# Sine arguments of a state-space mixer made in its front; one score product per head; softmax sums behind the scan; the exponential's table asked for before the score

## The reference, cut to what matters

```python
lam_bar = jnp.exp(lam * step)                      # one complex number per state
bu = jnp.einsum('blgh,gph->blgp', u_c, b_bar)
_, states = lax.associative_scan(_scan_combine, (a, bu), reverse=reverse, axis=1)
y = jnp.real(jnp.einsum('blgp,ghp->blgh', states, c))
...
s1 = jnp.einsum('bqhd,bkhd->bhqk', q_blk[..., 0, :], k1) + bias     # s2 alike
attn = jax.nn.softmax(s1, axis=-1) - lam * jax.nn.softmax(s2, axis=-1)
```

## Time and profile before

| what | us |
|---|---|
| median of 3 runs | 1440.96 |
| lowest and highest run | 1439.4, 1441.56 |
| span of the profiled execution, first to last instruction | 1437.0 |
| PE busy in the span | 1348.0 (94%) |
| DVE busy | 875.8 (61%) |
| ACT busy | 694.7 (48%) |
| POOL busy | 135.4 (9%) |

### The profile page before, as it was taken

One profiled execution on the slowest core, in us unless ns is written; L12 is line 12 of the kernel. 1 busy time (PEld: TensorE's weight loads), 2 busy tenths in 40 slices (PEclk: granted clock), 3 DMA queues, 4 the chain that ended last, 5 costly groups with the idle time before them and its releaser, 6 DMA issues.

```text
span 1437.0 us, 19125 instructions
## 1 busy us (share of the span) xinstructions
PE 1348.0 (94%) x7246; PEld 980.9 (68%) x7246; DVE 875.8 (61%) x1138; ACT 694.7 (48%) x1023; POOL 135.4 (9%) x111
## 2 busy tenths in 40 slices
PE   6996889999899779899999999999999999999996
PEld 6865558888787555776766667676766666666663
DVE  6888754454398875666565665555665555665552
ACT  4568443434246863445454544454444444444442
POOL 0455200000006640000000000000000000000000
PEclk9997999999899889899999999999999999999999
DMA  8541325443643126699999999999999999999993
GB/s 347 173 171 34 126 106 215 177 175 124 265 125 117 63 66 236 258 411 390 410 421 421 421 421 419 410 421 422 420 422 421 408 420 421 421 421 420 421 421 164
DMA packets 66329, 435.58 MB, mean 303 GB/s; under 512 B 8192, under 2 KB 14720, under 8 KB 16576
## 3 DMA queue, kind: packets, MB, share of 16 engines
q1 hardware_dynamic: 64848, 429.60, 74.4%
q0 software_dynamic: 1392, 4.78, 1.0%
HBM read 429.11 MB, written 2.10 MB: 300 GB/s over the span
## 4 chain that ended last, share of the span: by engine, by line
PE 73%; DMA 9%; DVE 9%; ACT 5%; SPq 2%; issue 2%; ACTq 0%; DVEq 0%
PE ps L2208 19%; PE ps L2243 11%; PE ps L2194 9%; PE ps L2096 7%; PE ps L1863 6%; PE ps L2225 6%; PE ps L2075 4%; DMA raw<-wmoe 4%; DMA first_ring<-wmoe 4%; PE ps L2001 2%; PE ps L1978 2%; SPq L548 2%; DVE raw L1321 1%; PE ps L1901 1%; PE ps L1989 1%
## 5 line engine op out<-in xcount | busy, mean ns | idle before, releaser
L2096 PE MATMUL ps<-wsplit,xh 128*128 128x512 f32 (+1 forms) x352 | 111.4, 388 | 5.0 <-DVE hv L1388 3.4
L1398 DVE TENSOR_TENSOR low_raw<-raw,last_uppers 128x2048 fp32r<-128x2048 f32 x39 | 89.2, 2289 | 38.5 <-ACT last_uppers L839 38.5
L1398 DVE TENSOR_TENSOR low_first<-first_ring,first_uppers 128x2048 fp32r<-128x2048 f32 x31 | 70.8, 2291 | 37.8 <-ACT first_uppers L839 37.8
L2243 PE MATMUL ps<-raw,hn 128*64 128x256 f32 x784 | 92.4, 382 | 0.0
L1863 PE MATMUL ps<-hT,mixw 128*128 128x256 f32 x384 | 89.4, 394 | 3.1 <-DMA mixw<-wmix 2.2
L1398 DVE TENSOR_TENSOR low_raw<-raw,first_uppers 128x2048 fp32r<-128x2048 f32 x31 | 70.8, 2289 | 32.6 <-ACT first_uppers L839 32.6
L1668 DVE TENSOR_TENSOR hv<-hv,ps 128x256 f32<-128x256 f32 x56 | 23.6, 421 | 105.3 <-ACT hv L989 105.3
L1362 DVE TENSOR_TENSOR wsplit<-raw,wsplit 128x2048 fp32r<-128x2048 f32 x33 | 74.5, 2289 | 20.1 <-ACT wsplit L798 20.1
L1863 PEld LDWEIGHTS ps<-hT,mixw 128*128 128x128 f32 x384 | 75.0, 198 | 15.2 <-issue 2.5
L2243 PE MATMUL ps<-last_ring,hn 128*64 128x256 f32 x704 | 83.2, 382 | 0.0
L989 ACT ACTIVATE hv<-ps 128x256 f32<-128x256 f32 x56 | 21.5, 384 | 127.5 <-PE ps L2208 127.5
(11 more groups left out here) (352 smaller groups left out, 3013.0 us busy)
## 6 DMA issues: line engine op xcount, KB each, us to landing
raw<-wmoe SPq DMA_DIRECT2D x148, 1024.0 KB, 22.4
first_ring<-wmoe SPq DMA_DIRECT2D x95, 1024.0 KB, 23.4
last_ring<-wmoe SPq DMA_DIRECT2D x91, 1024.0 KB, 23.2
raw<-wdense SPq DMA_DIRECT2D x33, 1024.0 KB, 5.0
mixw<-wmix SPq DMA_DIRECT2D x12, 2048.0 KB, 8.3
cyt<-bmat SPq DMA_DIRECT2D x2, 2048.0 KB, 12.1
cw<-cmat SPq DMA_DIRECT2D x2, 2048.0 KB, 18.4
qk<-wglu SPq DMA_DIRECT2D x2, 1024.0 KB, 5.0
```

What stands on the lines that cost most here:

```text
L1398: tt(lows[at], ring[at], uppers[k % UPPERS].bitcast(F32), ALU.subtract).then_inc(s["lo_done"], 1)
L2096: ins = mm(to, x2[:, fx, t * P:(t + 1) * P], of, start=(fx == 0 and i == 0), stop=(fx == KT - 1 and i == 2))
L2243: ins = mm(to, xlight[:, m % 2, fx], of[:, :, q * P:(q + 1) * P], start=(fx == 0), stop=(fx == KT - 1), tile_position=(0, LCAP * q))
```

## The change

It touches the mixer of both layers and nothing else.

1. The arguments of all 16 steps are made ahead of the loop, in four parts of 4, 4, 3 and 5 steps (`TURN_STEPS`): ACT's `phases` as two copies per step instead of four instructions, all 32 ahead of the eviction of zu1; one `nearest` per part (1024, 1024, 768, 1280 columns), and one `fracs` per part on DVE: part 0 ahead of `fold_c`, parts 1 and 2 behind it, part 3 in step 1. They lie in memory that v, hn and qk use later, and in a new tile `late`.
2. The shifted argument is gone: cos comes as the sine of (pi/2 - 2 pi |x|), so `trigs` is an Abs and three sines of 256 columns, the last behind a wait for the Abs.
3. `score` takes both least values of a head, then one product over 4 columns by a tensor_tensor with the slope from a column (four new memsets at the start), and gives one signal for both maps; `sums` multiplies by tensor_tensor too and stands behind the scan of its step.
4. ACT does a one-column exponential ahead of its wait for the score.
5. ACT waits for `frac_ready` in steps 1 and 2, and for `trig_ready` before the first eviction into v, because of the shared memory.

```diff
@@ -64,6 +64,7 @@
 STEPS = max(GP + 3, ATN_AT[-1] + 3)
+TURN_STEPS = (4, 4, 3, 5)
...
-        phase = sb("phase", [P, 2, SEQ])
-        turns = sb("turns", [P, 2, 2, SEQ])
+        late = sb("late", [P, 5, SEQ])
...
+        turn_parts = (v[:].rearrange("p t n -> p (t n)"), hn[:, 0], hn[:, 1, 0:3 * SEQ],
+                      late[:].rearrange("p i t -> p (i t)"))
+        whole_parts = [qk[:].rearrange("p a h t -> p (a h t)")[:, at:at + n * SEQ] for at, n in ((0, 4), (4 * SEQ, 4), (0, 3), (3 * SEQ, 5))]
...
@@ ScalarE @@
-            def phases(l, i):
-
-                n = GP * l + i
-                act.wait_ge(s["small_dve"], 2 * l + 2)
-                if n:
-                    act.wait_ge(s["frac_ready"], n)
-                for d in range(2):
-                    turn = small[:, 4, 2 * i + d:2 * i + d + 1]
-                    c = slice(d * NCH, (d + 1) * NCH)
-                    nc.scalar.activation(phase[:, 0, c], cst[:, C_T:C_T + NCH], ACT.Copy, scale=turn)
-                    ins = nc.scalar.activation(phase[:, 1, c], cst[:, C_T:C_T + NCH], ACT.Identity, bias=col[:, 17:18],
-                                               scale=turn)
...
+            def phases(l, b):
+
+                if b == 0:
+                    act.wait_ge(s["small_dve"], 2 * l + 2)
+                first = sum(TURN_STEPS[:b])
+                for i in range(first, first + TURN_STEPS[b]):
+                    for d in range(2):
+                        ins = nc.scalar.activation(turns_of(i)[:, d * NCH:(d + 1) * NCH], cst[:, C_T:C_T + NCH], ACT.Copy,
+                                                   scale=small[:, 4, 2 * i + d:2 * i + d + 1])
+                chain[0] += 1
+                phases_done[b] = chain[0]
+                ins.then_inc(s["act_chain"], 1)
+
+            def nearest(l, b):
+
+                act.wait_ge(s["act_chain"], phases_done[b])
+                if b >= 2:
+                    act.wait_ge(s["frac_ready"], len(TURN_STEPS) * l + b - 1)
+                nc.scalar.activation(whole_parts[b], turn_parts[b], ACT.Copy, bias=ROUND).then_inc(s["phase_ready"], 1)
...
-                nc.scalar.activation(trig[:, n % 3, 0], turns[:, i % 2, 1], ACT.Sin, scale=-TWOPI)
-                if between:
-                    between()
-                nc.scalar.activation(trig[:, n % 3, 1], turns[:, i % 2, 0], ACT.Sin, scale=-TWOPI)
-                nc.scalar.activation(trig[:, n % 3, 2], turns[:, i % 2, 0], ACT.Sin,
-                                     scale=TWOPI).then_inc(s["trig_ready"], 1)
+                chain[0] += 1
+                nc.scalar.activation(trig[:, n % 3, 0], turns_of(i), ACT.Abs).then_inc(s["act_chain"], 1)
+                nc.scalar.activation(trig[:, n % 3, 1], turns_of(i), ACT.Sin, scale=-TWOPI)
+                nc.scalar.activation(trig[:, n % 3, 2], turns_of(i), ACT.Sin, scale=TWOPI)
+                act.wait_ge(s["act_chain"], chain[0])
+                nc.scalar.activation(trig[:, n % 3, 0], trig[:, n % 3, 0], ACT.Sin, bias=col[:, 16:17],
+                                     scale=-TWOPI).then_inc(s["trig_ready"], 1)
...
                     if h >= 2:
                         full(unit(l, f"turn{h - 2}"))
+                    else:
+                        act.wait_ge(s["trig_ready"], GP * l + sum(TURN_STEPS[:h + 2]))
+                    nc.scalar.activation(col[:, 89:90], col[:, 17:18], ACT.Exp)
+                    act.wait_ge(s["score_ready"], HEADS * l + h + 1)
                     for m in range(2):
-                        act.wait_ge(s["score_ready"], 2 * (HEADS * l + h) + m + 1)
...
                 phases(l, 0)
+                phases(l, 1)
                 nearest(l, 0)
                 for k in range(2):
+                    if k:
+                        nearest(l, 1)
+                        phases(l, 2)
+                        phases(l, 3)
                     u = unit(l, "zu", k)
...
-                phases(l, 1)
-                trigs(l, 0, lambda: nearest(l, 1))
+                nearest(l, 2)
+                trigs(l, 0)
                 for i in range(STEPS):
-                    if i + 2 < GP:
-                        phases(l, i + 2)
-                        trigs(l, i + 1, lambda: nearest(l, i + 2))
-                    elif i + 1 < GP:
+                    if i + 1 < GP:
                         trigs(l, i + 1)
+                    if i == 0:
+                        nearest(l, 3)
+                    if i in (1, 2):
+                        act.wait_ge(s["frac_ready"], len(TURN_STEPS) * l + i + 2)
...
@@ VectorE @@
-            def fracs(l, i):
-
-                n = GP * l + i
-                dve.wait_ge(s["phase_ready"], n + 1)
-                stt(turns[:, i % 2], turns[:, i % 2], ROUND, phase[:], ALU.subtract,
-                        ALU.subtract).then_inc(s["frac_ready"], 1)
+            def fracs(l, b):
+
+                dve.wait_ge(s["phase_ready"], len(TURN_STEPS) * l + b + 1)
+                stt(turn_parts[b], whole_parts[b], ROUND, turn_parts[b], ALU.subtract,
+                    ALU.subtract).then_inc(s["frac_ready"], 1)
...
-            def score(l, h, m):
-
-                u = unit(l, f"map{h}.{m}")
-                full(u)
-                c, least = 64 + 4 * (h % 2) + 2 * m, col[:, 34 + 2 * m:36 + 2 * m]
-                at_least(dve, "score_ready", 2 * (HEADS * l + h) + m - 1)
-                link(nc.vector.tensor_reduce(least, ps[:, bank(u)].rearrange("p (a t) -> p a t", a=TT), axis=AX.X, op=ALU.min))
-                ts(col[:, c:c + 2], least, SLOPES[h], None, ALU.mult).then_inc(s["score_ready"], 1)
+            def score(l, h):
+
+                c = 64 + 4 * (h % 2)
+                at_least(dve, "score_ready", HEADS * l + h)
+                for m in range(2):
+                    u = unit(l, f"map{h}.{m}")
+                    full(u)
+                    ins = nc.vector.tensor_reduce(col[:, 34 + 2 * m:36 + 2 * m], ps[:, bank(u)].rearrange("p (a t) -> p a t", a=TT),
+                                                  axis=AX.X, op=ALU.min)
+                link(ins)
+                tt(col[:, c:c + 4], col[:, 34:38], col[:, 24 + h:25 + h].to_broadcast([P, 4]), ALU.mult).then_inc(s["score_ready"], 1)
...
-                ts(col[:, 82 + c:84 + c], col[:, 82 + c:84 + c], col[:, 14:15], None, ALU.mult).then_inc(s["sums_ready"], 1)
+                tt(col[:, 82 + c:84 + c], col[:, 82 + c:84 + c], col[:, 14:15].to_broadcast([P, 2]),
+                   ALU.mult).then_inc(s["sums_ready"], 1)
...
                 turn_b(l)
+                fracs(l, 0)
                 fold_c(l)
-                if l == 0:
-                    dve.wait_ge(s["in_cst"], 16)
-                fracs(l, 0)
                 fracs(l, 1)
+                fracs(l, 2)
                 stack = Stack(None)
                 for i in range(STEPS):
...
-                    for h in range(HEADS):
-                        if i == HEAD_AT[h] + T_SUMS:
-                            sums(l, h)
                     if i < GP:
                         rotate_in(l, i)
                         add_in(l, i)
                         scan(l, i)
-                    if i + 2 < GP:
-                        fracs(l, i + 2)
+                    for h in range(HEADS):
+                        if i == HEAD_AT[h] + T_SUMS:
+                            sums(l, h)
+                    if i == 1:
+                        fracs(l, 3)
```

More of the change, by code:

```diff
@@ L453, in at_least, with turn_part, turns_of @@
                 eng.wait_ge(s[what], n)
+        def turn_part(i):
+            return next(b for b in range(len(TURN_STEPS)) if i < sum(TURN_STEPS[:b + 1]))
+        def turns_of(i):
+            b = turn_part(i)
+            at = (i - sum(TURN_STEPS[:b])) * SEQ
+            return turn_parts[b][:, at:at + SEQ]
         @block.sync
@@ L718, in norm_empty @@
                     ins.then_inc(s["emptied_act"], 1)
-            def phases(l, i):
-                n = GP * l + i
-                act.wait_ge(s["small_dve"], 2 * l + 2)
-                if n:
-                    act.wait_ge(s["frac_ready"], n)
-                for d in range(2):
-                    turn = small[:, 4, 2 * i + d:2 * i + d + 1]
-                    c = slice(d * NCH, (d + 1) * NCH)
-                    nc.scalar.activation(phase[:, 0, c], cst[:, C_T:C_T + NCH], ACT.Copy, scale=turn)
-                    ins = nc.scalar.activation(phase[:, 1, c], cst[:, C_T:C_T + NCH], ACT.Identity, bias=col[:, 17:18],
-                                               scale=turn)
-                chain[0] += 1
-                ins.then_inc(s["act_chain"], 1)
@@ L735, in nearest @@
-            def nearest(l, i):
-                act.wait_ge(s["act_chain"], chain[0])
-                if GP * l + i >= 2:
-                    act.wait_ge(s["trig_ready"], GP * l + i - 1)
-                nc.scalar.activation(turns[:, i % 2], phase[:], ACT.Copy, bias=ROUND).then_inc(s["phase_ready"], 1)
-            def trigs(l, i, between=None):
-                n = GP * l + i
```

(17 more changed lines are left out.)

## The result

The changed kernel took 1435.56 us (median of seven runs, 1426.08 to 1438.02) against 1441.46 us before (seven runs, 1439.4 to 1449.35). By the medians the change is faster by 5.9 us where 17 were forecast, and 1435.56 lies above the range. Its own runs spread over 12 us, those of before, but for one, over 3; a second set of twelve runs of the same kernel gave 1432.46. The profiled execution ran 1436.12 us and its span is 1434.3, so it stands for the slower part of the runs, to which the median belongs.

A forecast was written before the change was run, and what follows sets the result against it. PE bounds each mixer's start (full to 104 us in layer 0), then DVE and ACT releasing each other up to the head norm. Layer gains 8.55 and 8.3, 16.85, called 17: median 1440.96 to 1424; range 1418 to 1430, full 1417 to 1432.

The forecast's parts named there:

- The front, a cost: Mixer start: PE begins 0.85 us late in layer 0, `local` 1.1 late in layer 1; bounds 0 to 2.5 a layer.
- I let all of it move with the end of the ring: Output projection, feed-forward and expert parts after the mixer: all start earlier by the mixer's gain, hiding none of it.
- The ring: Mixer steps up to the head norm, where DVE and ACT release each other's work: gains 8.55 us in layer 0, 8.3 in layer 1.
- To score(1): Mixer up to head 1's score: DVE stops being late and waits for PE's maps; 2.45 us gained, layer 0's late start included.
- Score(1) to score(2): Head 1's score to head 2's: 13.89 us falls to 11.1, gain 2.8, or 1.9 after 0.9 of waits beside POOL.
- Score(2) to rotation 13: Head 2's score to step 13's rotation: 10.56 us falls to 7.8, gain 2.75, less 0.6 of waits beside POOL.
- Rotation 13 to score(3): Step 13's rotation to head 3's score: 4.95 us falls to 3.46 without the subtraction, gain 1.5.
- Score(3) to the head norm: Head 3's score to the mixer's head norm: 12.54 us falls to 11.6, gain 0.95, less 0.4 of waits beside POOL.
- Holds: Score's and sums' new products on DVE wait beside POOL instructions: 0 to 1.27 us each, 1.9 a layer.
- Abs: Rival, in `trigs`: Abs outside sine's table adds two loads per `trigs`, 11 us a layer; 1446 us, chance 0.05.
- PE's order: Rival: both front delays fall on PE in each layer and the gain up to score(1) vanishes; 1429 us, chance 0.14.
- a ring held elsewhere: Rival, steps 10 to 15: POOL's pair ends last, about 13 us instead of 11 a pair; 1432 us, chance 0.12.

The follow-up runs named there:

- the gap filled: Changed kernel, with layer 1's second input product's eight matmuls repeated twice on PE, unread, ahead of the real ones: 1426.07 us, ratio 0.9902.
- the late C in the kernel before: Kernel before the change, with one of `fold_c`'s products made twice in layer 1 (2.2 us more DVE work): 1453.77 us, ratio 1.0108.
- C first: Changed kernel with part 0's subtraction moved behind `fold_c` in both layers: 1428.09 us, ratio 0.9924.
- the late C filled: Kernel before the change, with one `fold_c` product made twice in layer 1 and sixteen repeated input matmuls on PE: 1444.87 us, ratio 1.0037.
- Six dummies at the dense start: Changed kernel with part 0's subtraction behind `fold_c`, part 3's copies behind zu1's and B's evictions, six unread matmuls at the dense start: 1429.99 us.
- the head part: Kernel before the change, plus only one-product score, sums behind the scan and the exponential's load ahead: 1442.12 us, ratio 1.0018.
- the argument part alone: Changed kernel's new front and `trigs`, part 0 behind `fold_c`; score, sums and exponential's load as before the change: 1427.54 us, ratio 0.9916.

## Why the prediction was wrong

**The step that failed is "The front, a cost".** It priced C's delay as time: part 0's subtraction ahead of `fold_c`, 1.1 us. The delay is there: from the dense part's last addition to `local` layer 1 takes 37.4 us for 36.5, 0.9 more. But the step stopped at the start of `local`. Behind the input products PE was now idle for 1 to 2 us, its clock went from 2.4 to 1.2 GHz, and the next 20 us of a stretch in which PE is full cost 9.6 us. The bound of 2.5 us a layer took in only delays. Three experiments carry this: the gap filled (8.55 us fewer from `local` to the head norm, C as late), the late C in the kernel before (11.4 us for 2.2), and the same filled (9.9 us back). In layer 1 the clock fell in each of the five profiled executions in which PE waited 0.99 us or more between the input products and `local`: 1.99, 1.07, 0.99, 1.93 and 1.32 us. In layer 0 gaps of 0.35 and 0.43 us there did nothing.

**"I let all of it move with the end of the ring"** failed in a smaller way. From head norm to the dense part's last addition 2.5 us were lost to a start at half clock behind an unchanged gap of 3.3 us, and 1.6 us went in the expert part. Both come in the filled kernel too: there the lead is 7.9 us at the first head norm, 6.6 at the addition, 5.1 at `local`, 13.8 at the second head norm and 12.1 at the end. So without the large fall the sum of 17 would still have come out at 12 in that execution, at 14.8 in that of "C first", and at 14.2 by the medians of the filled kernel and of before. That these falls belong to the clock is shown by the rows; that the change causes them is not. The slow dense start stands in all eight profiled executions with the arguments in the front and nothing added there, but of the four without them it stands in one, the late C filled (7.16 us for 5.70 to 5.73), whose layer 0 is that of before; and the slow products of the expert part are in the kernel before as well. Six dummies at the dense start removed that one.

**The ring was right.** From `local` to the head norm layer 0 takes 93.5 us for 102.8, 9.3 less, where the terms give 8.55 and the front's 0.85, 9.4. To score(1): 1.52 from the span's start, or 3.2 after `local`, for 2.45 and 0.85. Score(1) to score(2): 2.33 for 1.9. Score(2) to rotation 13: 2.57 for 2.15. Rotation 13 to score(3): 1.49 for 1.5. Score(3) to the head norm: 0.3 lost for 0.55 gained, for the product was held 1.19 us at 127.69 and DVE waited 0.85 for the last sines. The total agrees better than its terms: two stretches gained 0.4 us each beyond their terms, and the last made up for it by 0.9. Without a fall layer 1's ring, in the filled kernel, is 94.6 for 103.3.

**The split of the gain was wrong.** The forecast credits the exponential's load with part of each stretch. Alone the head part gave 0.9 us in layer 0 and 1.5 in layer 1, and no measurable time; the argument part alone gave 7.8 of the 9.3.

**The front in layer 0.** `local` began 1.7 us late and zu1's eviction, at 32.66, 1.9 late, where 0.85 was forecast; ACT began 0.9 later (20.75 for 19.87) because the constants landed later in that execution, and the remaining 1.0 is the forecast's term. In "C first", where the same copies stand ahead of it, PE began its products at 42.28, 0.1 earlier than before: the term is smaller than what executions differ by.

**Holds were right in kind and in size**: the product of score took 0.161 us at least, 1.212 at most, and the one at 127.69 stands beside POOL. From score(1) on the holds in layer 0 come to 1.8 us (0.95 for 0.18 at 110.30, 1.19 for 0.17 at 127.69), where 1.9 was forecast, though in other stretches. The Trainium skill, GPSIMD Engine Reference, Specifications, names two SBUF inputs as a case of contention; the exchange back to tensor_scalar, which has one, took the same time, so no run here shows that the number of inputs matters for instructions this small. **Abs** brought no load:

```profile
120.05 0.43 ACT L761 ACTIVATE trig<-late 128x256 f32<-128x256 f32 x1
120.49 1.28 ACT L762 ACT_TABLE_LOAD   x1
121.78 0.42 ACT L762 ACTIVATE trig<-late 128x256 f32<-128x256 f32 x1
```

The one load stands between Abs and the sine, where exponentials came before, and the sine follows it after 1.29 us: a switch costs the load and no drain, as the sum had it. The two rivals on PE's order and on a ring held elsewhere (1429 and 1432) came nearest in time and were wrong in mechanism: PE's order gained its 1.5 us, and from score(1) to the head norm DVE's longest wait, 2.76 us, is put down to ACT's sines, none of DVE's or ACT's to POOL.

The prediction's own list of signs held the clue, "an expert part that grows by what the mixers lost", but named a longer part, not a slower clock; that the windows show 0.80 in the ring's thin stretch should have led to the question what a new gap on PE does. Two slips bear on nothing: the 0.402 us at 256 columns is a sine's row, not a copy's, and the low end of the full range, no holds and no front, comes to 1418.4 by its own terms, not 1417.

What stays open: why some executions of one kernel fall and others not. The gap behind the input products divides the profiled executions in layer 1, but PE's idle time altogether does so nearly as well, and no experiment tells the two apart. From 400 us to `local` it is 3.23, 1.71, 2.23, 2.99 and 2.56 us in the five executions that fell, the 1.24 us at 403.35 among it, and 0 to 1.70 in the nine that did not; in layer 0, from 28 us on, it is 1.86 where the clock fell and at most 1.80 elsewhere. Only one pair speaks for the place of the gap: 1.71 us of which 1.07 stood behind the products fell, and 1.70 ahead of them did not. The repeats take away both, so they can't decide it. And the smaller falls were bought off one at a time; each time another turned up.

## What to carry to other kernels

When an edit makes a full PE wait, price two things: the wait, and its next stretch at 1.2 GHz. Here 1 to 2 us of idle time behind a short burst of products cost 9 us more, and 3.3 us elsewhere cost nothing, or 1.4 to 2.7. Read the granted clock around each place where the change moves a producer of PE's operands, and put DVE work that nothing waits for behind the work PE waits for. Where the producer can't be earlier, a few repeated matmuls ahead of the wait cost little, no more than they outlast the idle time (0.1 to 1.9 us here).

## What the hardware showed that was not expected

Gaps of 1 to 2 us on PE were followed by 17 to 20 us at granted clock 0.50, in a kernel whose PE is busy 95% of the span. The length of the last gap alone does not decide: the clock fell behind 0.99 us, with another wait of 1.24 us some 13 us earlier, it stayed behind 1.70 us ahead of the input products in one execution, and it fell behind 1.86 there in another. And a delay of 2.2 us on VectorE made the kernel before 13.5 us slower, six times its size, which sixteen matmuls that compute nothing of use brought down to 3.6.
